# Rotary embedding of the first block by VectorE's 32-lane shuffle, queries' roots as softmax scale

## The reference, cut to what matters

```python
h = rms_norm(x, norm1_w[l]) * (1.0 + scale1) + shift1
proj = h @ w_in[l]
q, k, v, xBC, z, dt_raw, gates = jnp.split(proj, offsets, axis=-1)
q = rms_norm(q.reshape(b, s, N_Q_HEADS, HEAD_DIM), q_norm_w[l])
k = rms_norm(k.reshape(b, s, N_KV_HEADS, HEAD_DIM), k_norm_w[l])
v = v.reshape(b, s, N_KV_HEADS, HEAD_DIM)
q = axial_rope(q, cos_r, sin_r, cos_c, sin_c)
k = axial_rope(k, cos_r, sin_r, cos_c, sin_c)
attn = block_attention(q, k, v)
ssd = ssd_mixer(xBC, z, dt_raw, conv_w[l], conv_b[l], A_log[l], dt_bias[l], ssd_D[l], ssd_norm_w[l])
```

## Time and profile before

| | us |
|---|---|
| three timed runs | 948.18, 947.74, 932.56 |
| their median | 947.74 |
| the profiled execution | 935.42 |
| its span in the trace | 933.6 |

### The profile page before, as it was taken

One profiled execution on the slowest core, in us unless ns is written; L12 is line 12 of the kernel. 1 busy time (PEld: TensorE's weight loads), 2 busy tenths in 40 slices (PEclk: granted clock), 3 DMA queues, 4 the chain that ended last, 5 costly groups with the idle time before them and its releaser, 6 DMA issues.

```text
span 933.6 us, 18288 instructions
## 1 busy us (share of the span) xinstructions
PE 910.7 (98%) x7536; PEld 873.6 (94%) x7536; DVE 666.9 (71%) x915; ACT 506.5 (54%) x686; POOL 92.8 (10%) x66
## 2 busy tenths in 40 slices
PE   4999999999999999999999999999999999999998
PEld 4899999879888889999999999999998999999998
DVE  6755899888689998877876645545786676666642
ACT  2374654656787786344655543445468564445431
POOL 0000155120056523000000000000000000000000
PEclk9998999999999999999999999999999999999999
DMA  9765454566632224566665555546241246565660
GB/s 375 267 226 181 136 172 145 205 208 219 208 110 91 91 91 169 205 261 223 231 233 191 183 201 203 186 165 215 95 157 65 100 142 212 189 207 188 225 204 23
DMA packets 25085, 168.01 MB, mean 180 GB/s; under 512 B 2868, under 2 KB 4532, under 8 KB 5048
## 3 DMA queue, kind: packets, MB, share of 16 engines
q1 hardware_dynamic: 23760, 164.90, 50.8%
q10 hardware_dynamic: 1256, 2.12, 0.7%
HBM read 165.95 MB, written 1.06 MB: 179 GB/s over the span
## 4 chain that ended last, share of the span: by engine, by line
PE 88%; DVE 5%; ACT 3%; DMA 2%; issue 1%; SPq 0%; DVEq 0%; ACTq 0%
PE bank L1807 86%; DVE acc L1116 2%; DMA adas<-w_stream 1%; DVE cvt L1271 1%; DVE wlo L1074 1%; ACT whi L570 1%; PE bank L2058 1%; DMA raw<-w_stream 1%; PE bank L2082 0%; ACT kw__111 L803 0%; PE bank L2346 0%; PE bank L2386 0%; DVE sp L1596 0%; ACT cvt L676 0%; ACT prob L706 0%
## 5 line engine op out<-in xcount | busy, mean ns | idle before, releaser
L1807 PE MATMUL bank<-hhi,whi 128*128 128x256 f32 (+1 forms) x1364 | 388.6, 286 | 0.1
L1074 DVE TENSOR_TENSOR wlo<-raw,whi 128x2048 fp32r<-128x2048 f32 (+1 forms) x131 | 300.4, 2293 | 112.6 <-ACT whi L570 110.4
L1807 PE MATMUL bank<-hlo,whi 128*128 128x256 f32 (+1 forms) x1352 | 377.1, 279 | 0.0
L1807 PE MATMUL bank<-hhi,wlo 128*128 128x256 f32 (+1 forms) x1352 | 377.0, 279 | 0.0
L570 ACT ACTIVATE whi<-raw 128x2048 fp32r<-128x2048 f32 (+1 forms) x132 | 250.9, 1901 | 95.6 <-PE bank L1807 71.3
L1807 PEld LDWEIGHTS bank<-hhi,whi 128*128 128x128 f32 (+1 forms) x1364 | 257.0, 189 | 7.0 <-issue 6.0
L1807 PEld LDWEIGHTS bank<-hlo,whi 128*128 128x128 f32 (+1 forms) x1352 | 255.3, 189 | 0.9 <-issue 0.6
L1807 PEld LDWEIGHTS bank<-hhi,wlo 128*128 128x128 f32 (+1 forms) x1352 | 255.9, 189 | 0.0
L1807 PE MATMUL bank<-fhi,wlo 128*128 128x256 f32 x432 | 119.5, 277 | 0.0
L1807 PE MATMUL bank<-flo,whi 128*128 128x256 f32 x432 | 119.4, 276 | 0.0
L1807 PE MATMUL bank<-fhi,whi 128*128 128x256 f32 x432 | 119.4, 276 | 0.0
(11 more groups left out here) (289 smaller groups left out, 1359.1 us busy)
## 6 DMA issues: line engine op xcount, KB each, us to landing
raw<-w_stream SPq DMA_DIRECT2D x147, 1024.0 KB, 5.0
adas<-w_stream SPq DMA_DIRECT2D x8, 1024.0 KB, 8.7
xres<-x_t SPq DMA_DIRECT2D x1, 1024.0 KB, 10.2
out<-oute SPq DMA_DIRECT2D x8, 128.0 KB, 4.0
tabs<-tabs_in_dram ACTq DMA_DIRECT2D x1, 641.0 KB, 4.5
tabs<-tabs_in_dram ACTq DMA_DIRECT2D x1, 512.0 KB, 3.9
hankel<-bucket_rows ACTq DMA_DIRECT2D x1, 512.0 KB, 5.9
cols<-cols_in_dram ACTq DMA_DIRECT2D x1, 325.0 KB, 8.2
```

Source lines behind the costliest of these rows:

```text
L1074: nc.vector.tensor_tensor(out=wlo[:, c % RING, 0:n], in0=raw[:, r % RING, 0:n], in1=whi[:, c % RING, 0:n].bitcast(f32), op=ALU.subtract)\
L1807: return nc.tensor.matmul(out, lhsT, rhs, start=start, stop=stop)
```

## The change

The head sums of the queries are made right away, four per q chunk between its halves (`query_sums`); the keys' sums are two matmuls whose stationary operand repeats one column of `half` 64 times, so that they come out spread over features (`key_sums`). The squares are read from PSUM, and the evictions multiply by the norm's weights. Roots are taken as exponential of minus half the logarithm (`head_logarithms`, `head_roots`). The queries are never multiplied by their roots: these go into the softmax as the `scale` operand of the exponentials and into the shift (`shifts`). Only the keys are multiplied, in one instruction. The rotation acts on unnormalised pairs of blocks (128 x 512) in the query stage: VectorE permutes the partitions by 16 within each 32 (`stream_shuffle`), one product applies sign and sine, GpSimd does cosines and sum, five pairs in all. `swap`, `head_spread`, `block_norm`, `rqx` and the matmuls behind them are gone from the first block. Some small work moves: ScalarE's copies for `vtok` and `csr` from xbc 0 to xbc 1 and 2, VectorE's difference for `csr` and the decays from xbc 0 to xbc 3, the values' transposes from xbc 0 to xbc 1. The bank of a q or k chunk counts as empty when it is squared.

```diff
-        uses("q", 6, qkv_out)
+        uses("q", 5, qsq_done)
+        emptied.append((qkv_out, 6))
...
-                nc.scalar.activation(dst.rearrange("p a t -> p (a t)"), both(USE["q"] + i), ACT.Copy)\
-                  .then_inc(qkv_out, 1)
+                weight = 1.0 if i == 5 else col("kw") if i == 4 else qw8[:, 0:1]
+                nc.scalar.activation(dst.rearrange("p a t -> p (a t)"), both(USE["q"] + i), ACT.Copy,
+                                     scale=weight).then_inc(qkv_out, 1)
...
+            def head_logarithms():
+
+                act.wait_ge(qss_done, 2)
+                nc.scalar.activation(qroot[:, :, :], side[0][:, 0:2 * 16].rearrange("p (t h) -> p t h", t=NT),
+                                     ACT.Ln, bias=epsc[:, 0:1], scale=1.0 / HD).then_inc(qroot_done, 1)
+                nc.scalar.activation(kroot[:, :, :].rearrange("p a t -> p (a t)"), side[1][:, :], ACT.Ln,
+                                     bias=epsc[:, 0:1], scale=1.0 / HD).then_inc(qroot_done, 1)
+
+            def head_roots():
+
+                act.wait_ge(qroot_done, 2)
+                nc.scalar.activation(kroot[:, :, :], kroot[:, :, :], ACT.Exp, scale=-0.5).then_inc(rqx_done, 1)
+                nc.scalar.activation(qroot[:, :, :], qroot[:, :, :], ACT.Exp, scale=-0.5).then_inc(rq_done, 1)
...
                                          ACT.Exp, bias=smax[:, h % 4, t:t + 1],
+                                         scale=qroot[:, t, h:h + 1],
...
+            SWAP = [16 + j for j in range(16)] + list(range(16))
+
+            def rotation(p):
+                dve.wait_ge(qkv_out, p + 1)
+                if p == 0:
+                    dve.wait_ge(tabs_in, 16)
+                    step(nc.vector.tensor_reduce(sign[:, :], tab("swap"), AX.X, ALU.add, negate=True))
+                if p >= 2:
+                    dve.wait_ge(qrot_done, p - 1)
+                turned_pair = rot1[:, p % 2, :, :]
+                step(nc.vector.stream_shuffle(turned_pair.rearrange("p a t -> p (a t)"),
+                                         rope_pair(p).rearrange("p a t -> p (a t)"), SWAP))
+                after()
+                nc.vector.scalar_tensor_tensor(out=turned_pair, in0=turned_pair, scalar=sign[:, :],
+                                               in1=spread(tab("sin"), 1, 2), op0=ALU.mult, op1=ALU.mult)\
+                  .then_inc(qsin_done, 1)
...
+                if i >= 1:
+                    rotation(i - 1)
...
-                if i >= 3:
-                    block_norm(i - 3)
                 split(FIRST["xbc"] + i + AHEAD)
-                if i >= 4:
-                    rotation(i - 4)
-                if i == 11:
-                    block_norm(9)
+                if i == 1:
+                    dve.wait_ge(rqx_done, 1)
+                    dve.wait_ge(qrot_done, 5)
+                    nc.vector.tensor_tensor(out=rope_pair(4), in0=rope_pair(4), in1=kroot[:, :, :], op=ALU.mult)\
+                      .then_inc(qn_done, 1)
...
+            def shifts(j):
+                dve.wait_ge(max_done, 2 * j + 2)
+                dve.wait_ge(rq_done, 1)
+                top = smax[:, 2 * j % 4:2 * j % 4 + 2, :]
+                nc.vector.tensor_tensor(out=top, in0=top, in1=qroot[:, :, 2 * j:2 * j + 2].rearrange("p t h -> p h t"),
+                                        op=ALU.mult).then_inc(shift_done, 1)
...
+            def query_sums(j):
+
+                pe.wait_ge(tabs_in, 16)
+                pe.wait_ge(qsq_done, j + 1)
+                for t in range(NT):
+                    for b in range(2):
+                        at = 16 * t + 4 * j + 2 * b
+                        last = mm(side[0][:, at:at + 2], sqq[:, 2 + 2 * j + b, t * P:(t + 1) * P], tab("half"))
+                if j == 3:
+                    last.then_inc(qss_done, 1)
+
+            def key_sums():
+
+                pe.wait_ge(qsq_done, 5)
+                for part in range(2):
+                    one = tab("half")[:, part:part + 1]
+                    last = mm(side[1][part * HD:(part + 1) * HD, :],
+                              bass.AP(tensor=one.tensor, offset=one.offset, ap=[list(one.ap[0]), [0, HD]]),
+                              sqq[:, 0:2, :])
+                last.then_inc(qss_done, 1)
...
             for i in range(12):
                 half("xbc", i, 0, hhi, hlo)
-                if i >= 2:
-                    if i == 2:
-                        pe.wait_ge(rqx_done, 1)
-                    head_spread(i - 2, 0, rqx, side[1 + i % 2])
-                half("xbc", i, 1, hhi, hlo, None, head_squares(0, sqq, 10, 0) if i == 0 else None)
-                if i >= 3:
-                    swap(i - 3)
-                if i == 0:
+                if i == 1:
                     pe.wait_ge(qkv_out, 6)
```

More of the change, by code:

```diff
@@ L514, in _ @@
             pool.wait_ge(tabs_in, 16)
-            rope(0)
-            for n in range(10):
-                if n < 9:
-                    rope(n + 1)
-                rotated(n)
-            pool.wait_ge(qrot_done, 10)
+            for p in range(5):
+                rope(p)
+                rotated(p)
+            pool.wait_ge(qrot_done, 5)
+            pool.wait_ge(qn_done, 1)
             pool.wait_ge(dec_done, 1)
@@ L655, in _ @@
                     nc.scalar.activation(aneg[:, :], col("alog", 0, 2 * NH), ACT.Exp).then_inc(dtl_done, 1)
-                if i == 5:
+            def head_logarithms():
[8 more added lines that the diff above has]
+                nc.scalar.activation(qroot[:, :, :], qroot[:, :, :], ACT.Exp, scale=-0.5).then_inc(rq_done, 1)
+            for i in range(13):
+                c = FIRST["xbc"] + i
+                if i < 12:
+                    split(c + AHEAD)
+                if i == 0:
+                    head_logarithms()
                     act.wait_ge(dsum_done, 1)
@@ L659, in _ @@
                         "p (t h) -> p t h", t=NT), ACT.Exp).then_inc(dexp_done, 1)
-            for i in range(13):
-                c = FIRST["xbc"] + i
-                if i == 1:
-                    act.wait_ge(rq_done, 1)
-                    nc.scalar.activation(rqx[:, :, :, :], spread(rq[:, :, :], 3, HD), ACT.Copy)\
-                      .then_inc(rqx_done, 1)
+                    head_roots()
                 if i < 12:
-                    split(c + AHEAD)
                     out_of(c)
@@ L1333, in _ @@
                 if i == 0:
-                    rotation(8)
-                    rotation(9)
                     maxima(0)
                     maxima(1)
+                    shifts(0)
                     normalised(0)
@@ L1342, in _ @@
                     maxima(3)
+                    shifts(1)
                 split(FIRST["z"] + i + AHEAD)
@@ L2035, in _ @@
                     last.then_inc(vt_done, 1)
+                half("xbc", i, 1, hhi, hlo)
             def scores_pair(j):
                 kb = head(2 * j)[2]
-                pe.wait_ge(qrot_done, j + 3)
+                if j == 0:
+                    pe.wait_ge(qrot_done, 5)
+                    pe.wait_ge(qn_done, 1)
+                    pe.wait_ge(qroot_done, 2)
                 if j >= 1:
```

109 lines of the change are left out of this document (44 added, 65 removed).

## The result

The changed kernel took a median of 934.1 us (22 runs, 926.03 to 941.36), the kernel before 941.78 us (22 runs, 932.56 to 949.41): ratio 0.992, 95% interval 0.990 to 0.994. So it is faster by 7 to 8 us: the interval tells that from no change, but it is less than the 2% at which a change of this kernel is called faster. The forecast was a gain of 10.9 us that ends at 924.5.

What follows compares the result with a forecast made beforehand. TensorE, busy 98% of 933.6 us, bounds the kernel, with VectorE the next limit. Convolution 11 ends 15.5 us earlier from t0, less 4.8 added and 0.2 net other work: 935.4 - 10.9 = 924.5 us, forecast 921 to 928, range 918 to 938.

Steps and rivals of the forecast that it cites:

- The base: Whole kernel: the profiled execution of before, 935.42 us, from which the gain of 10.9 us was subtracted.
- rival at 937: Whole kernel: the long product step is the common one, same gain from 947.7, ending at 937; chance 0.2.
- 10.9 us at z 3: At z 3, behind VectorE's lead: convolution 11 ends 10.7 us earlier, other small work nets 0.2, gain 10.9 us.
- t0 + 4.8: Query stage: four head-sum groups (3.8 us) and the keys' sums (1.0) move the start of xbc 0 4.8 us later.
- The clock drop, 3.3 us: At the 20 head sums, about 86 to 94 us: TensorE's half clock before the change costs 3.3 us.
- ScalarE's chain and the two loads: Ahead of convolution 0: two table loads of 1.28 us among ScalarE's work; taps end at t0 + 7.7, convolution 1.3 us late.
- TensorE's waits for convolutions 3 and 4, 2.0 us: In xbc: VectorE's extra pieces make TensorE lose 2.0 us in all by xbc 6, nothing more after.
- VectorE 5.34 and TensorE 5.44 a chunk: In xbc after convolution 4: work per chunk, TensorE's 5.44 us a little more than VectorE's 5.34.
- the xbc stage keeps 0.118: In xbc: long product step, 1.1 us less gain; with other losses the kernel ends at 928 to 931; chance 0.13.
- The wait ahead of z 3: In z 0 to z 3: VectorE leads and TensorE still waits for normalised probabilities, 2.15 us at 195.87 before.
- z 0 to z 3 tighten: In z 0 to z 3: the 2.15 us wait and a 1.7 us clock drop go, about 920; chance 0.12.
- the rival that ends slower: Query stage: each of five new groups of small sums drops the clock, 3.3 us each, ending at 941; chance 0.04.

Runs made afterwards that it cites:

- the third: Third set of timed runs, both kernels unchanged: changed kernel median 928.46 us (6 runs) against 941.08 of before (11), ratio 0.990 (0.984 to 0.996).
- Experiment 2: Kernel before with the 20 head sums in five groups of four in chunks q 1 to v, none in xbc 0: 944.31 us, ratio 1.003.
- the first and fourth profiles: Profiled executions of the changed kernel, nothing edited: spans 934.0 and 937.2 us, changed stage 107.2 and 107.3 us.

## Why the prediction was right or wrong, point by point

- **The base (wrong).** "Sum: the profiled execution took 935.42; 935.4 - 10.9 = 924.5": the step that failed is the first term of this sum. It stood for a typical execution of before, and it measured 941.78 (the median of 22 runs), 6.4 us more; only one of the 22, 932.56, is below 935.42. The profiled execution had the short step in both long stretches and no drop in the second block, while the long stretches of before took the long step in seven of ten. The text named the cause (3120 products at 0.0047 us; the two long stretches show 2883 products and 12.7 us) and even gave it a rival at 937, but counted the low value as the likelier from one profile and one run of three. Of the 9.6 us between 924.5 and 934.1 the base makes 6.4, and the gain between the medians, 7.7 instead of 10.9, makes 3.2. The rival at 937 lies within 3 us, in part by luck: its base, 947.74, was 6.0 too high, and its gain 3.2. 941.8 - 10.9 would have been 930.9, against the 934.1 measured in this set and 928.46 in the third. An execution of the same kind as the base did come out at 927.03, 924.4 without its clock drop.
- **The size of the gain (right in the stage, not all of it seen in the times).** Forecast 10.9 us at z 3; the stage gave 10.6 over nine profiles. Between the medians there are 7.7, 7.5 and 12.6 us, between the means 8.3. A part can be the clock drop in the second block, which lengthens the attention part beyond 95.1 us by 2.1 us on average over the ten profiles of the changed kernel and its versions and by 1.1 over the seven of before and its versions; with that scatter it is not shown, and the missing 2 us stay open.
- **What was added in the query stage: t0 + 4.8 (right).** xbc 0 begins at 81.9 us after and about 78.3 before, and the query stage began 1.1 us earlier: + 4.7.
- **The clock drop, 3.3 us (right that it goes, wrong as a term by itself).** Experiment 2 moved only the sums, lost the drop and gained nothing at the scores; among the profiles of before the drop goes with 0.4 to 2.6 us of the stage. It did no harm to the total, since z 0's place was worked out from both engines' chains and not from this term.
- **ScalarE's chain and the two loads (right).** The taps end 7.9 us after t0 (forecast 7.7), and the first convolution starts late as said. The loads at L663 and L682, 1.28 us each, are both there. By the rule of the Trainium skill (ScalarE: Activation LUTs, Table sets: the hidden batching unit) one of them would be missing; this trace does not agree.
- **TensorE's waits for convolutions 3 and 4, 2.0 us (right).** 1.6 us in three places.
- **VectorE 5.34 and TensorE 5.44 a chunk (right).** 5.32 for VectorE, and 5.44 or, by execution, 5.65 for TensorE; that the engines are nearly level was the point. The rival "the xbc stage keeps 0.118" is what the first and fourth profiles show in their last chunks, for 1.3 us (107.2 against 105.9).
- **Shuffles at nothing (right).** 0.73 us each, the product behind it 0.75. Beside GpSimd that product took 0.99 (79.93), still under cover.
- **The wait ahead of z 3 (right that it stays, its size off).** It is 0.85 us at 186.35 instead of 2.15, while the one ahead of z 2 grew from 1.39 to 2.31, and the clock now drops behind that one; the two together take 3.2 us instead of 3.5. GpSimd's row products now fall on the normalisation that TensorE waits for at 186.35, which takes 3.70 us for the pair that takes 0.62 alone (the rows below), and no longer on the accumulations of the earlier trace rows. The rival "z 0 to z 3 tighten" did not happen: scores to `so` 201.1 before, 201.1 after.
- **Exponentials with their scale operand (a size off).** 0.56 us for 128x256 against 0.47 with one operand less; taken as unchanged. That they lie under VectorE's lead was argued and is not shown by a run.
- **The clock in the query stage (right).** 1.00 behind each group of four; the rival that ends slower is out.

The rows of the collision, GpSimd and VectorE after:

```profile
182.11 4.03 POOL L457 TENSOR_TENSOR bd<-csr,dsel 128x1024 fp32r<-128x1024 f32 x2 [98.60 <-ACT zt L768]
```

```profile
176.81 0.62 DVE L1347 TENSOR_SCALAR prob<-prob,srec 128x256 f32<-128x256 f32 x2
...
182.59 3.70 DVE L1347 TENSOR_SCALAR prob<-prob,srec 128x256 f32<-128x256 f32 x2
```

And the exponentials, after and before:

```profile
157.97 0.56 ACT L719 ACTIVATE prob<-bank,smax,qroot 128x256 f32<-128x256 f32 x1
```

```profile
168.34 0.47 ACT L706 ACTIVATE prob<-bank,smax 128x256 f32<-128x256 f32 x1
```

## What to carry to other kernels

Before a difference is subtracted from a profiled time, see where that execution stands among the runs: if the median is far above it, the forecast is the median less the gain, and the profile is for the gain alone. Compare two profiles stage by stage between the same two instructions, and lay aside first the stretches in which nothing was changed; here they moved by more than the change did. And a clock drop or a stall on the busiest engine is worth little by itself if another engine's chain ends at nearly the same place: take it away alone and see what is waited for next.

## What the runs showed of the hardware

- The same row of 128x256 products runs at 0.1132 or 0.1177 us each at a fully granted clock; a stretch keeps its step, and which it has changes from one execution of the same kernel to the next (short in 3 and long in 7 of ten long stretches of before, 4 and 4 of eight after). 1380 products cost 156.4 or 162.5 us.
- The granted clock falls to 0.50 (1.2 GHz of 2.4) behind small products in some executions and not in others. In the attention part of the second block it fell, in the 17 profiles of all kernels here, behind the head sums in eight (1.2 to 2.6 us above 95.1), behind the 48 small products of weights and values in three (4.2 to 4.4 us above it), and in six not at all.
- A shuffle of 128x512 f32 within 32 lanes takes 0.73 us on VectorE with a mask load of 0.01, and a pair of 128x256 scalings takes 0.62 us alone and 3.70 beside GpSimd's products of 128x1024.
